# Hybrid decoder layer: hi and lo of the sample tokens in one stationary operand, first two FFN products between the transposes, value products after the gate piece

## The chip, the cores and the metric

The kernel runs on one core of one Trainium2 chip. The metric is device time in microseconds of one launch. TensorE (PE) multiplies matrices into the 8 banks of PSUM; VectorE (DVE), ScalarE (ACT) and GpSimd (POOL) do elementwise work; SyncE's queue (SP) issues most transfers.

## The reference, cut to what matters

One layer over 1024 prompt tokens and 64 sample tokens, D = 1024, all in float32:

```python
x = layer_norm(ALPHA * x + 0.5 * swiglu(x, ffn_wi[0], ffn_wo[0]), ln_g[0], ln_b[0])
q_a, k_a, v_a, q_r, k_r, v_r, g_r, gate_a, gate_b = split(x @ w_in)
o_a = sliding_window_attention(rope(q_a), rope(k_a), v_a, sinks)        # 8 query heads, window 128
o_r = group_norm(retention(rope(q_r), rope(k_r), v_r)) * silu(g_r)      # 4 heads, chunks of 128
merged = sigmoid(gate_a) * (o_a @ w_br_attn) + sigmoid(gate_b) * (o_r @ w_br_ret)
x = layer_norm(ALPHA * x + merged @ w_o, ln_g[1], ln_b[1])
x = layer_norm(ALPHA * x + 0.5 * swiglu(x, ffn_wi[1], ffn_wo[1]), ln_g[2], ln_b[2])
```

`swiglu(x, wi, wo)` is `(silu(x @ wi[:, :F]) * (x @ wi[:, F:])) @ wo` with F = 2816. The sample tokens have a cache and a state of their own and share all weights.

## The kernel before, in words

Matrix products in float32 accuracy are made of three reduced-precision matmuls: both operands are split into a high part (a rounding copy, on ScalarE) and a low part (the difference, on VectorE), and `three` (L1790) issues hi by hi, hi by lo and lo by hi into one bank. So each operand costs ScalarE and VectorE a step, and each product TensorE three passes.

The order of work is written out by hand on every engine, and engines meet by semaphores. Three parts follow each other.

FFN 0 (`ffn(0)` on each engine). The tokens are two halves of 512 (tile p and tile p+4), D is two halves too, and each up projection is seven products of half-size blocks instead of eight (a Strassen-like scheme). Seven blocks of x are needed, numbers 0 to 6: 0, 2 and 6 are parts of x, and 4, 3, 1, 5 are sums that GpSimd makes in `tm` (`combos`, L705). In the head TensorE transposes them p by p (`combos`, L1809, 28 groups of four 128x128 transposes), ScalarE copies the high part, VectorE makes the low part, all through rotating banks. `sample_combos` does the 64 sample tokens. Then come 11 units g of seven products (`up_product`, L1861; two banks of 12 matmuls of 512 columns each), whose results VectorE and ScalarE combine to the two halves of the hidden layer (`up_step`), while `w_hi`, `w_lo` and `w_sum` split and add the weights for the product three ahead in three slots. In unit 0 product 0 uses wa11, product 1 the sum ws2 and product 2 wa12. The sample tokens of products 0, 2, 4 and 5 already use a stationary operand of hi and lo side by side (`sample_product`), added afterwards by a product with `fold`. The hidden layer is spilled, and 77 down steps follow.

The mixer goes over three groups G of tokens: tiles 0 to 2, 3 to 5, and 6, 7 and the 64 sample rows. `build_timeline` lists its stages: P (q, k, v of one retention head, 4 weight pieces), G and G2 (its gate), TR (transposes of q and k), SKV, PVQ, SU (states), T, B (branch product), GB and GA (gates, a piece each, transposed), KVA and QA (attention's projections), AS (scores), EX, FIN (softmax), AP (transposes of the probabilities), AV (value products), A (branch), WO (output product, 2 pieces, added into y by VectorE), LNS and LNH (LayerNorm's statistics; the scaled rows). Weight pieces pass through three raw slots and four split slots (`Pace`). P, G, KVA and QA are `token_major` (L1986): the tokens are the stationary operand, and the third tile of group 2 has only 64 columns.

FFN 1 repeats FFN 0. All engines wait for the last WO piece before it; TensorE waits also for all its additions (`wacc_done`). Its x comes from LayerNorm 1, whose affines of tiles 6, 7 and 8 are VectorE's (`affine`, L1164) and stand between its low parts; those of tiles 0 to 5 are GpSimd's and are done within groups 1 and 2.

## Time and profile before

| | us |
|---|---|
| median of 3 runs (2507.74 to 2508.51) | 2508.28 |
| the profiled execution | 2506.91 |
| its span | 2505.1 |
| TensorE busy | 2434.7 (97%) |
| VectorE busy | 1652.3 (66%) |
| ScalarE busy | 902.5 (36%) |
| GpSimd busy | 232.5 (9%) |

FFN 0 takes the span to about 742 us, the mixer to 1740.6, FFN 1 the rest. A row of a timeline gives start, time, engine, line, operation, out<-in, shapes and, in brackets, how long the engine was idle before it and what released it. A shape `128*64 128x512` is a stationary operand of 128 rows and 64 columns, and 512 moving columns. A matmul's time is a modelled end, the distance of two starts is the pace. Starts are in us from the span's begin.

### The profile page before, as it was taken

To read this page: it belongs to the slowest core of one execution; us is meant where nothing else is said; L and a number is where in the kernel's file an instruction comes from. 1 tells how busy PE (TensorE), PEld (TensorE's weight loads), DVE (VectorE), ACT (ScalarE), POOL (GpSimd) and SP (SyncE) were. 2 spreads that over 40 slices of the span, in tenths; PEclk is the share of its full clock that TensorE was granted. 3 is DMA by queue.
4 is the path that set the end of the run, shared out by engine and by line. 5 is a ranking of instruction groups with operands and counts; after the bars stand their busy time and mean duration, and the time that the engine had idled before them with its cause. 6 is when DMAs were issued, how large, how long until landed. Compare 5 with 4: busy or idle time off the path is not lost.

```text
span 2505.1 us, 31982 instructions
## 1 busy us (share of the span) xinstructions
PE 2434.7 (97%) x12781; PEld 2078.1 (83%) x12781; DVE 1652.3 (66%) x2249; ACT 902.5 (36%) x1280; POOL 232.5 (9%) x306
## 2 busy tenths in 40 slices
PE   7999999999999999999999999998799999999997
PEld 6888888888888898988989778887688888888886
DVE  5666565657886657675666766566765666555788
ACT  4222222243353337442355322373322222224344
POOL 3000000000021000030000221201300000000011
PEclk9999999999999999999999999999899999999999
DMA  4232222266444333333333445424123222227643
GB/s 140 85 120 81 94 80 96 94 225 208 147 138 126 93 101 115 105 114 118 93 115 102 127 128 173 148 85 143 55 84 106 84 105 81 93 85 232 200 147 126
DMA packets 225571, 300.09 MB, mean 120 GB/s; under 512 B 13392, under 2 KB 166272, under 8 KB 222592
## 3 DMA queue, kind: packets, MB, share of 16 engines
q1 hardware_dynamic: 211792, 240.43, 30.4%
q0 software_dynamic: 13056, 56.48, 6.1%
q8 instruction: 101, 1.65, 0.3%
q10 hardware_dynamic: 576, 1.15, 0.1%
q14 instruction: 46, 0.38, 0.0%
HBM read 243.81 MB, written 55.18 MB: 119 GB/s over the span
## 4 chain that ended last, share of the span: by engine, by line
PE 85%; DVE 6%; ACT 3%; issue 2%; POOL 2%; DMA 1%; SPq 0%; DVEq 0%; ACTq 0%; POOLq 0%
PE ps L1794 25%; PE ps L1795 25%; PE ps L1796 25%; PE ps L1849 2%; PE ps L1850 2%; DMA b_raw<-in_ffn_wo 1%; PE ps L1930 1%; PE ps L1931 1%; ACT prob L1075 1%; DVE w_lo L445 1%; ACT w_hi L439 1%; PE ps L1858 1%; DVE b_lo L1253 1%; PE ps L2224 1%; PE ps L2089 0%
## 5 line engine op out<-in xcount | busy, mean ns | idle before, releaser
L1794 PE MATMUL ps<-xc_hi,u_hi 128*128 128x512 f32 x1232 | 483.4, 392 | 0.0
L1795 PE MATMUL ps<-xc_lo,u_hi 128*128 128x512 f32 x1232 | 480.6, 390 | 0.0
L1796 PE MATMUL ps<-xc_hi,u_lo 128*128 128x512 f32 x1232 | 480.1, 390 | 0.0
L445 DVE TENSOR_TENSOR w_lo<-raw,w_hi 128x1024 fp32r<-128x1024 f32 x198 | 253.7, 1295 | 139.8 <-ACT w_hi L439 139.6
L1796 PEld LDWEIGHTS ps<-xc_hi,u_lo 128*128 128x128 f32 x1232 | 231.6, 188 | 49.3
L1794 PEld LDWEIGHTS ps<-xc_hi,u_hi 128*128 128x128 f32 x1232 | 232.0, 188 | 46.1 <-issue 0.2
L1795 PEld LDWEIGHTS ps<-xc_lo,u_hi 128*128 128x128 f32 x1232 | 232.0, 188 | 45.2
L439 ACT ACTIVATE w_hi<-raw 128x1024 fp32r<-128x1024 f32 x198 | 205.7, 1055 | 170.0 <-PE ps L1796 144.8
L1794 PE MATMUL ps<-w_hi,xg_hi 128*128 128x512 f32 (+1 forms) x720 | 246.4, 342 | 1.7 <-issue 1.7
L1794 PE MATMUL ps<-b_hi,h_hi 128*128 128x512 f32 x616 | 241.4, 392 | 2.6 <-DVE b_lo L1253 2.6
L1795 PE MATMUL ps<-w_lo,xg_hi 128*128 128x512 f32 (+1 forms) x720 | 242.0, 336 | 0.0
L1796 PE MATMUL ps<-w_hi,xg_lo 128*128 128x512 f32 (+1 forms) x720 | 241.5, 335 | 0.0
L1796 PE MATMUL ps<-b_hi,h_lo 128*128 128x512 f32 x616 | 239.8, 389 | 0.0
L1795 PE MATMUL ps<-b_lo,h_hi 128*128 128x512 f32 x616 | 239.7, 389 | 0.0
L835 ACT ACTIVATE u_hi<-wa 128x1024 fp32r<-128x1024 f32 x88 | 93.1, 1058 | 303.5 <-PE ps L1850 224.0
L881 ACT ACTIVATE h_hi<-h_raw 128x512 fp32r<-128x512 f32 x154 | 97.3, 632 | 269.6 <-PE ps L1796 185.7
L1213 DVE TENSOR_TENSOR u_lo<-wa,u_hi 128x1024 fp32r<-128x1024 f32 x88 | 109.6, 1246 | 96.8 <-ACT u_hi L835 96.7
L1252 DVE TENSOR_TENSOR h_lo<-h_raw,h_hi 128x512 fp32r<-128x512 f32 x154 | 105.7, 686 | 70.4 <-ACT b_hi L835 70.1
L1794 PEld LDWEIGHTS ps<-w_hi,xg_hi 128*128 128x128 f32 x720 | 131.8, 183 | 20.5 <-issue 3.7
L1796 PEld LDWEIGHTS ps<-w_hi,xg_lo 128*128 128x128 f32 x720 | 131.8, 183 | 17.0
L1795 PEld LDWEIGHTS ps<-w_lo,xg_hi 128*128 128x128 f32 x720 | 131.9, 183 | 16.2
L1794 PEld LDWEIGHTS ps<-b_hi,h_hi 128*128 128x128 f32 x616 | 115.6, 188 | 31.9 <-DVE b_lo L1253 6.6
(289 smaller groups left out, 4451.9 us busy)
## 6 DMA issues: line engine op xcount, KB each, us to landing
raw<-in_w_in SPq DMA_DIRECT2D x90, 512.0 KB, 3.8
wa<-in_ffn_wi SPq DMA_DIRECT2D x88, 512.0 KB, 3.6
h_raw<-h_spill SPq DMA_DIRECT2D x154, 256.0 KB, 2.8
h_spill<-tm POOLq DMA_DIRECT2D x22, 1024.0 KB, 4.1
b_raw<-in_ffn_wo SPq DMA_DIRECT2D x66, 256.0 KB, 3.8
raw<-in_w_in SPq DMA_DIRECT2D x96, 128.0 KB, 2.3
raw<-in_w_in SPq DMA_DIRECT2D x48, 256.0 KB, 3.0
raw<-in_w_br_ret SPq DMA_DIRECT2D x24, 512.0 KB, 3.7
```

The costliest lines, as they stand in the source:

```text
L439: nc.scalar.activation(wslot(n, False), raw[:, s * D:(s + 1) * D], ACT.Copy).then_inc(hi_ready, 1)
L445: nc.vector.tensor_tensor(wslot(n, True), raw[:, s * D:(s + 1) * D], fr(wslot(n, False)), ALU.subtract).then_inc(lo_ready, 1)
L835: nc.scalar.activation(dst, src, ACT.Copy).then_inc(sem_, 1)
L881: nc.scalar.activation(h_hi[s][:], h_raw[s][:], ACT.Copy)
L1075: ins = nc.scalar.activation(pb[:, q * wd:(q + 1) * wd], pb[:, q * wd:(q + 1) * wd], ACT.Exp, bias=nmx[:, s0 + q:s0 + q + 1], accum_out=rs ...
L1213: tt(u_lo[s][:], w_src[i][:], fr(u_hi[s][:]), ALU.subtract).then_inc(u_dve, 1)
L1252: tt(h_lo[s][:], h_raw[s][:], fr(h_hi[s][:]), ALU.subtract)
L1794: mm(out, a_hi, b_hi, start=first, stop=False)
L1795: mm(out, a_hi, b_lo, start=False, stop=False)
L1796: return mm(out, a_lo, b_hi, start=False, stop=last)
L1849: mm(out, lhs, u_hi[s][:, k * 2 * P:(k + 1) * 2 * P], start=first and k == 0, stop=False)
L1850: ins = mm(out, lhs, u_lo[s][:, k * 2 * P:(k + 1) * 2 * P], start=False, stop=last and k == 3)
```

## The change

1. Sample pairs in the mixer. The split x of the sample tile gets its low part also beside the high part (columns 64 to 127 of `xg_hi`, likewise `mT_hi`). `token_major` and WO then issue two matmuls with these 128 columns (by the high and by the low weights), and rows 64 to 127 of the bank are added to rows 0 to 63 by VectorE: `fold_halves`, a copy and an addition, ahead of each use of the sample rows in P, G2, KVA, QA; in WO a second addition. The copy of v in P is made tile by tile behind `rope_src`, and for the sample rows by VectorE.
2. FFN heads. The blocks are now 0, 1 and 6 as parts of x (p, second half is block 1) and 4, 3, 2, 5 as sums; product 1 uses wa12 and product 2 the sum ws2. Blocks 0 and 1 are "early", the others "late", each kind with banks of its own. In FFN 0 the head is the order `HEADS[0]`: E early, L late blocks of p, U one half (12 matmuls) of product 0 or 1. GpSimd's sums have two sets of buffers and wait only for those of p-2. The sample products of 0 and 1 come in the middle of product 2. Loads come in a new order.
3. FFN 1. The early blocks are stages EB of the timeline between the WO stages of group 2, with the first weight split as UW; GpSimd's sums for p of 0 and 1 are made there. LayerNorm's statistics follow each addition of the last WO. The head is `HEADS[1]`, with `affine(1, 6)`, `(1, 7)` and `(1, 8)` behind low parts.
4. AV stands behind the gate piece and EX; in group 0 the four affine steps of P stand ahead of the weight splits.
5. Buffers lie elsewhere in SBUF, with the waits that this needs; one is in the load of down step 2.

```diff
-BLOCKS = (0, 2, 6, 4, 3, 1, 5)
+EARLY = (0, 1)
+LATE = (6, 4, 3, 2, 5)
+HEADS = ((("E", 0), ("E", 1), ("L", 0), ("E", 2), ("E", 3), ("L", 1), ("U", 0), ("U", 1), ("L", 2), ("U", 2), ("U", 3), ("L", 3)),
+         (("E", 0), ("E", 1), ("E", 2), ("E", 3), ("U", 0), ("L", 0), ("U", 1), ("L", 1), ("U", 2), ("U", 3), ("L", 2), ("L", 3)))
+E_BANKS, L_BANKS = (0, 1, 3, 4), (4, 5, 6, 7)
...
-            s += [("AS", u + 2), ("AV", u)] + gate() + [("EX", u + 2)]
+            s += [("AS", u + 2)] + gate() + [("EX", u + 2), ("AV", u)]
...
-        s += [("WO", 1), ("WO", 2), ("WO", 3)] + [("LNS", t) for t in range(3)] + [("LNH", t) for t in range(3)]
+        s += [("WO", 1), ("EB", 0), ("EB", 1), ("WO", 2), ("EB", 2), ("EB", 3), ("UW", 0), ("WO", 3)]
...
+                if t == 2:
+                    sp.wait_ge(prod_done, product(f, UNITS - 1, 6))
...
-                if p:
-                    pool.wait_ge(xb_done, 28 * f + 7 * p)
+                if p >= 2:
+                    pool.wait_ge(xb_done, blocks_made(f, LATE[-1], p - 2))
...
-                if k and kind != "WO" and (kind, x) not in (("A", 0), ("A", 1), ("A", 2)):
-                    pace.stage(n, k)
                 if G == 0 and (kind, x) in (("P", 1), ("P", 2), ("P", 3)):
                     for t in ((NT - 1, 4), (5, 6), (7,))[x - 1]:
                         affine_scale(0, t)
                         affine_shift(0, t)
+                if k and kind != "WO" and (kind, x) not in (("A", 0), ("A", 1), ("A", 2)):
+                    pace.stage(n, k)
...
+            def fold_halves(dst, b, off, n):
+                lo, hi = halves(b, off, n)
+                link(nc.vector.tensor_copy(dst, lo))
+                return tt(dst, dst, hi, ALU.add)
...
+                    for t in range(3 if G < NG - 1 else 2):
+                        R = rows_of(3 * G + t)
+                        act.wait_ge(rope_src, 3 * g + t + 1)
+                        dst = v_r[0:R, (3 * (g % 2) + t) * DV:(3 * (g % 2) + t + 1) * DV]
+                        ins = nc.scalar.activation(dst, bank(t, R, 2 * DK, DV), ACT.Copy)
...
+                        if R == SR:
+                            fold_halves(v_r[0:SR, (3 * (g % 2) + 2) * DV:(3 * (g % 2) + 3) * DV], t, 2 * DK, DV)
+                            src = tA[0:SR, 2 * DK:4 * DK]
+                            link(fold_halves(src, t, 0, 2 * DK))
...
+                            if R == SR:
+                                out, pair = bank(b0 + t, P, 0, width), xg_hi[:, a:a + 2 * SR]
+                                mm(out, pair, wh[:, kk * width:(kk + 1) * width], start=k == 0, stop=False)
+                                ins = mm(out, pair, wl[:, kk * width:(kk + 1) * width], start=False, stop=k == KT - 1)
+                                continue
...
+                        ins = stt(ysl, ysl, ALPHA if x == 0 else 1.0, bank(b, R), ALU.mult, ALU.add)
+                        if R == SR:
+                            link(ins)
+                            ins = tt(ysl, ysl, halves(b, 0, BANK)[1], ALU.add)
+                        ins.then_inc(wacc_done, 1)
+                        if last_group and x == 3:
+                            dve.wait_ge(wacc_done, 24 * G + 18 + q + 1)
+                            ins = nc.vector.bn_stats(st6[0:R, 12 * t + 6 * (q % 2):12 * t + 6 * (q % 2) + 6], ysl)
...
+                else:
+                    late(f, 0)
+                    w_lo(f, 0, 1)
                     affine(1, 6)
+                    late(f, 1)
                     affine(1, 7)
...
+                w_sum(f, 0, 0)
+                late(f, 2)
+                late(f, 3)
+                w_lo(f, 0, 2)
+                first_gate(f)
                 if f:
                     affine(1, 8)
...
+            def head(f):
+                for kind, x in HEADS[f]:
+                    if kind == "E" and f == 0:
+                        early(f, x)
+                    elif kind == "L":
+                        late(f, x)
+                    elif kind == "U":
+                        first_half(f, x // 2, x % 2)
+                sample_combos(f)
+                pe.wait_ge(xb_lo, 28 * (f + 1))
```

## Rows read from the trace of the kernel before

**Rows 1.** The page: busy time of TensorE, share of the span, instructions.

```profile
PE 2434.7 (97%) x12781; PEld 2078.1 (83%) x12781; DVE 1652.3 (66%) x2249; ACT 902.5 (36%) x1280; POOL 232.5 (9%) x306
```

**Rows 2.** Busy times by stretch: us, then PE, PEld, DVE, ACT, POOL, granted clock, DMA.

```profile
6.30:31.90 25.60, 19.62 (x121) 17.03 (x121) 19.60 (x28) 16.53 (x29) 20.98 (x16) 0.87 0.59 202
1401.00:1740.60 339.60, 332.11 (x2095) 276.70 (x2095) 214.62 (x355) 128.84 (x201) 56.76 (x67) 0.98 0.45 140
1740.60:1795.50 54.90, 35.11 (x176) 29.09 (x177) 44.58 (x55) 25.11 (x40) 27.99 (x25) 0.81 0.14 44
```

**Rows 3.** Waits of TensorE, whole span: us in total, times, longest.

```profile
PE ps L2224 <- ACT probT L1086: 6.3, 7, 2.5
...
PE ps L2053 <- ACT v_r L993: 4.4, 3, 1.5
```

**Rows 4.** TensorE by form in 1401 to 1741, the hi-by-hi third: busy us, mean ns.

```profile
L1794 PE MATMUL ps<-w_hi,xg_hi 128*64 128x512 f32 x40 | 15.9, 397 | 0.0
...
L1794 PE MATMUL ps<-w_hi,xg_hi 128*64 128x256 f32 x40 | 11.1, 277 | 0.0
...
L1794 PE MATMUL ps<-w_hi,mT_hi 128*64 128x512 f32 x16 | 6.3, 393 | 0.0
```

**Rows 5.** Timeline of TensorE, group 2, end of P(0) and begin of its transposes.

```profile
1416.76 0.39 PE L1796 MATMUL ps<-w_hi,xg_lo 128*128 128x512 f32 x1
1416.98 0.40 PE L1794 MATMUL ps<-w_hi,xg_hi 128*64 128x512 f32 x1
1417.22 0.39 PE L1795 MATMUL ps<-w_lo,xg_hi 128*64 128x512 f32 x1
...
1421.80 0.28 PE L1796 MATMUL ps<-w_hi,xg_lo 128*64 128x256 f32 x1
1421.92 0.84 PE L2053 MATMUL ps<-ident,qk 128*128 128x128 f32 x4
```

**Rows 6.** Timeline of VectorE in group 2: sample rows of P(0), a state update, WO.

```profile
1419.23 0.41 DVE L1501 TENSOR_TENSOR tA<-ps,cs_ret 64x256 f32<-64x256 f32 x1
1419.57 0.41 DVE L1502 TENSOR_TENSOR tB<-ps,cs_ret 64x256 f32<-64x256 f32 x1
...
1501.18 1.22 DVE L1619 SCALAR_TENSOR_TENSOR st<-st,ps 128x1024 f32<-128x1024 f32 x1 [1.45 <-PE ps L2115]
...
1739.24 0.68 DVE L1163 SCALAR_TENSOR_TENSOR y<-y,ps 64x512 f32<-64x512 f32 x1 [0.69 <-PE ps L1796]
```

**Rows 7.** Timeline of ScalarE in the attention of group 2.

```profile
1648.92 1.00 ACT L1086 ACTIVATE probT<-ps 128x1024 f32<-128x1024 f32 x1
1649.94 1.28 ACT L1032 ACT_TABLE_LOAD   x1
...
1656.02 1.00 ACT L1086 ACTIVATE probT<-ps 128x1024 f32<-128x1024 f32 x1
```

**Rows 8.** Waits of TensorE in 760 to 900.

```profile
PE ps L1794 <- DVE racc L1637: 1.6, 1, 1.6
```

**Rows 9.** Timeline of VectorE in P(1) of group 0.

```profile
784.99 1.23 DVE L445 TENSOR_TENSOR w_lo<-raw,w_hi 128x1024 fp32r<-128x1024 f32 x1 [2.85 <-ACT w_hi L439]
786.13 1.21 DVE L1184 TENSOR_TENSOR y<-y,ln_g_down 64x1024 f32<-64x1024 f32 x1
```

**Rows 10.** Timeline of TensorE: product 2 of FFN 0, WO(2), product 2 of FFN 1.

```profile
45.29 0.39 PE L1794 MATMUL ps<-xc_hi,u_hi 128*128 128x512 f32 x1
...
1724.02 0.39 PE L1794 MATMUL ps<-w_hi,mT_hi 128*128 128x512 f32 x1
...
1795.55 0.39 PE L1794 MATMUL ps<-xc_hi,u_hi 128*128 128x512 f32 x1
```

**Rows 11.** Timeline of GpSimd: a sum in each FFN head.

```profile
7.46 1.28 POOL L722 TENSOR_TENSOR tm<-y 128x512 f32<-128x512 f32 x1
...
1754.46 2.29 POOL L722 TENSOR_TENSOR tm<-y 128x512 f32<-128x512 f32 x1
```

**Rows 12.** Timeline of VectorE: affine of tiles 6 and 7 in the second head.

```profile
1754.41 1.22 DVE L1174 TENSOR_TENSOR y<-y,ln_g_mix 128x1024 f32<-128x1024 f32 x1
...
1757.76 2.28 DVE L1174 TENSOR_TENSOR y<-y,ln_g_mix 128x1024 f32<-128x1024 f32 x1
```

More of the change, by code:

```diff
@@ L184, in slot_of, with block_order, block_place, blocks_made @@
     return n % MSLOTS
+def block_order(f):
+    return [(ci, p) for kind, p in HEADS[f] for ci in {"E": EARLY, "L": LATE, "U": ()}[kind]]
+def block_place(f, ci, p):
+    return block_order(f).index((ci, p))
+def blocks_made(f, ci, p=None):
+    return 28 * f + 1 + max(block_place(f, ci, u) for u in (range(4) if p is None else (p,)))
+def block_bank(ci, p):
+    return E_BANKS[(2 * p + ci) % 4] if ci in EARLY else L_BANKS[(5 * p + LATE.index(ci)) % 4]
+def bank_freed(f, ci, p):
+    n = block_place(f, ci, p)
+    same = [m for m, (c2, p2) in enumerate(block_order(f)[:n]) if block_bank(c2, p2) == block_bank(ci, p)]
+    return 28 * f + same[-1] + 1 if same else 0
 def product(f, g, i):
@@ L501, in down_bank, with halves @@
             return (4 * q + i) % 7
+        def halves(b, off, n):
+            return bank(b, SR, off, n), ps[SR:2 * SR, b * BANK + off:b * BANK + off + n]
         def sample_heads(dst):
@@ L1151, in xT_evac @@
                 lo = dst_lo[:].rearrange("p (k c) -> p k c", c=width)[:, :, col:col + R]
-                tt(lo, pair, hi, ALU.subtract).then_inc(xT_lo_ready, 1)
+                ins = tt(lo, pair, hi, ALU.subtract)
+                if R == SR:
+                    beside = dst_hi[:].rearrange("p (k c) -> p k c", c=width)[:, :, col + SR:col + 2 * SR]
+                    ins = tt(beside, pair, hi, ALU.subtract)
+                ins.then_inc(xT_lo_ready, 1)
             def ln_stats(t):
@@ L1491, in _, with rope @@
             nc.vector.memset(va_prev[:], 0.0).then_inc(prev_zeroed, 1)
-            def rope(G, R, src, t, cs, half, heads, dst1, dst2):
+            def fold_halves(dst, b, off, n):
+                lo, hi = halves(b, off, n)
+                link(nc.vector.tensor_copy(dst, lo))
+                return tt(dst, dst, hi, ALU.add)
+            def rope(G, R, src, t, cs, half, heads, nth=0):
                 cos = cs[0:R, t * 2 * half:t * 2 * half + half]
@@ new lines, in early, with late, first_half @@
+            def early(f, p):
+                if f and p == 0:
+                    pe.wait_ge(m_ready, KT * NG)
+                for ci in EARLY:
+                    block(f, ci, p)
+            def late(f, p):
+                if f and p == 0:
+                    pe.wait_ge(wacc_done, 24 * NG)
+                for ci in LATE:
+                    block(f, ci, p)
+            def first_half(f, i, half):
+                if half == 0:
+                    pe.wait_ge(u_dve, weight_op(f, 0, LO_AT[i]))
+                    pe.wait_ge(xb_lo, blocks_made(f, i))
+                    if f and i == 0:
+                        pe.wait_ge(wacc_done, 24 * (NG - 1) + 21)
+                b = (2, 0)[i] + half
+                for k in range(4):
+                    c0 = k * 2 * P + half * P
+                    xs = slice(k * HALF, (k + 1) * HALF)
+                    ins = three(bank(b), u_hi[i][:, c0:c0 + P], u_lo[i][:, c0:c0 + P],
+                                xc_hi[i][:, xs], xc_lo[i][:, xs], k == 0, k == 3)
+                if half:
+                    ins.then_inc(main_done, 1)
@@ L1891, in up_product @@
                                     xc_hi[i][:, xs], xc_lo[i][:, xs], k == 0, k == 3)
[L1892 to L1893 removed]
+                    if g == 0 and i == 2 and j == 0:
+                        pe.wait_ge(xs_dve, 4 * f + 4)
+                        for first in range(2):
+                            sample_product(f, 0, first).then_inc(prod_done, 1)
+                if i in (0, 1, 4, 5):
+                    if i == 0:
                         pe.wait_ge(fs_ready, u)
[L1895 to L1897 removed]
                     ins = sample_product(f, g, i)
@@ L2301, in _ @@
                             a = mb + f2 * TG + t * P
+                            if R == SR:
+                                out, pair = bank([2, 5, 6, 7][(6 * x + q) % 4]), mT_hi[:, a:a + 2 * SR]
+                                mm(out, pair, wslot(n + f2, False)[:, half * 512:(half + 1) * 512], start=f2 == 0, stop=False)
+                                ins = mm(out, pair, wslot(n + f2, True)[:, half * 512:(half + 1) * 512], start=False, stop=f2 == 1)
+                                continue
                             ins = three(bank([2, 5, 6, 7][(6 * x + q) % 4], R), mT_hi[:, a:a + R], mT_lo[:, a:a + R],
@@ L2307, in _ @@
                     ins.then_inc(piece_used, 2)
-            pe.wait_ge(wacc_done, 24 * NG)
+                elif kind == "EB":
+                    early(1, x)
             ffn(1)
```

370 lines of the change are left out of this document (224 added, 146 removed).

## Prediction, made before the result was known

> **What bounds the kernel now.** I read the page's busy shares first, then busy times by stretch, then TensorE's waits, then the engines' own timelines inside the stretches with gaps. TensorE is busy 97% of the span [rows 1], so time can be saved in two ways: fewer TensorE instructions, or its gaps. The gaps are few. The waits name them [rows 3]: the value products of the attention wait for the copy of the transposed probabilities (6.3 us), the retention transposes for the value copy (4.4 us), and the rest lies mostly in the two FFN heads. By stretch [rows 2], the first head (6.3 to 31.9) has TensorE busy 19.6 of 25.6 us; the second with its first two products (1740.6 to 1795.5) 35.1 of 54.9 us at a granted clock of 0.81 (a mean of stretches at 1.2 and at 2.4 GHz). Group 2 of the mixer (1401 to 1740.6) is the opposite: 332 of 339.6 us busy, VectorE 215 of them. There a removed TensorE instruction counts in full, and what is added to VectorE has room.
>
> **A. Sample pairs (group 2).** Each k of the 64 sample columns now takes three matmuls (hi by hi, lo by hi, hi by lo). The change puts hi and lo side by side as 128 stationary columns and does it in two. By form there are 40 triples 512 wide (four P stages and QA), 40 of 256 (G, G2, KVA) and 16 in WO [rows 4]. The width of the stationary operand doesn't show in the pace: with 128 columns the next matmul starts after 0.22 us, with 64 after 0.24, and at 256 wide after 0.12 [rows 5]; I take 0.23 and 0.12. Saved: 40 x 0.23 + 40 x 0.12 + 16 x 0.23 = 17.7 us.
> The price is on VectorE: the two halves of PSUM are added, a copy and an addition for each tile, of 64 rows. The nearest rows are 0.41 us for 64x256, starting 0.34 apart, and 0.68 for 64x512 [rows 6]. P gets four such steps with four linked waits, about 1.9 us ahead of the third rope. At head 0 only the G piece stands between P and the transposes: P ends near 1417.6, the transposes begin at 1421.9 [rows 5], and the third rope, of 1.3 us, began at 1419.23 [rows 6], with TensorE's stretch between them shorter by 4 x 0.12 us afterwards. I put 1.2 us of stall there. In the other heads the row product and its sample half also lie between (6 us of room). The fold behind G2 (0.8 us) falls into the 1.45 us in which VectorE waits for the state product [rows 6]. KVA, QA and the transposes of x have a stage between them and their readers. Bounds of the stall: nothing, and 3 us if every sample evacuation leaked a little. A = 17.7 - 1.2 = 16.5 (14.5 to 17.7).
>
> **B. Value products behind the gate.** AP, AS, AV, gate, becomes AP, AS, gate, AV. The gate (3.5 us in group 2) covers ScalarE's copy. But ScalarE is the limit there in group 2: between its copies at 1648.92 and 1656.02, 7.1 us, its rows name no idle time, and two table loads of 1.28 us lie there [rows 7]; TensorE's work in such a round is some 6.3 us, worked out from its starts. What the gate hides at the first units comes back in part at AV of the last, when the copy is behind the sample's exponentials (about 1.2 us). Of 3.8 us of gaps in group 2 I keep 2.6, in groups 0 and 1, with longer gates, 1.5 each. B = 5.6; bounds 0 (all given back to ScalarE's chain) and 7.2 (all gaps).
>
> **C. Group 0: affines ahead of the splits, value copies tile by tile.** In P(1) VectorE does four affine steps of 1.21 us from 786.13 on, after the last weight split and before the first rope [rows 9], so the transposes wait. Ahead of the splits they have P's 16 us to hide in; the split they delay (772.4 to 778.4) is used at 783.4. That ends two of the three 1.5 us waits, and the third (head 0) gets 0.8 from the earlier copy. With VectorE 4.9 us earlier some of the branch products' wait for racc (1.6, [rows 8]) goes, I take 0.8. C = 1.6 + 1.6 + 0.8 + 0.8 = 4.8; bounds 1.5 and 6.5.
>
> **D. First FFN head.** Now: 112 transposes in 13.7 us of TensorE time and 6 us of gaps, product 0, a wait for the sample's low parts, its sample product, product 1; product 2 starts at 45.3 [rows 10]. Then: the four halves of products 0 and 1 (12 x 0.23 = 2.7 us each) lie between the blocks. GpSimd's 16 sums (1.28 each, starting 1.25 apart from 6.2, [rows 11]) end near 28 to 30, since they no longer wait for buffers. TensorE: E0 to L1 until about 18.7, U0 and U1 to 24.2, L2 26.6, U2 and U3 32.0, L3 34.4; low parts and the split of ws2 behind it until 36.9. Product 2 starts at 37, one more sample product (1.1 us) comes after it, and the wait for the sample's low parts (until about 40.7, half a product in at 39.7) costs 1.0. Saved 45.3 - 39.1 = 6.2 at most. If the low clock falls into products and not, as now, on transposes (before: a mean of 0.87 in the head [rows 2]), up to 3.4 us of work at half pace go off. D = 5; bounds 1 and 8.
>
> **E. Second FFN head.** The eight early blocks move into WO (32 transposes, 3.7 us of TensorE), LayerNorm's statistics into the last WO, and four halves of products fill the wait for LayerNorm. From the end of WO(1) (1724.0) to product 2 (1795.55) are 71.5 us now [rows 10]. The new limit is VectorE. Behind WO(1) I count on it: 12 additions of 0.62, 4 second halves, 4 splits, 8 early low parts, one u_lo, six statistics; it ends 26.5 us after WO(1), some 7 us after TensorE, which waits 2.9 us before L0. Then five low parts 3.3, u_lo 1.2, affine of 6 2.4, five 3.2, affine of 7 2.4, two weight sums 2.5, ten low parts 6.5, u_lo 1.2, first gate 1.2, affine of 8 2.4: 26.3. GpSimd's sums for p of 2 and 3 cannot start before those affines. Where both engines ran from SBUF in the trace, VectorE's affine took 2.28 us where it is 1.22 alone and GpSimd's sum 2.29 where it is 1.28 [rows 11, 12]; low parts, which read PSUM, kept their 0.6 in the same stretch. That adds 1.6 + 2 us, and the first blocks of L0 and of the last L some 1. Product 2 starts 57.8 us after WO(1); with one more sample product and 0.7 of stall 59.5, so 12.0 us less, of which 1.8 are A's. TensorE idles about 8 us just before product 2; before, its clock was at 1.2 GHz after gaps of 5.3, 4.9 and 2.35 us, and product 1 began at half pace. I take off 2.2. E = 12.0 - 1.8 - 2.2 = 8; bounds 2 and 14.
> The Trainium skill's page "SBUF — State Buffer", section "SBUF: two separate sides", has a rule against this part: a VectorE instruction with two SBUF inputs and a GpSimd one exclude each other for the whole instruction. The rows agree with about one instruction's wait for each meeting. If every one of the five VectorE instructions beside the sums waited once more, E would be 6 and not 8.
>
> **What costs nothing.** In the units g of 1 and above products 1 and 2 swap roles; banks, sums and splits are as many, and TensorE is full there now. The wait put before the load of down step 2 holds SyncE's queue until product 5 of the last unit is through; the step is used 5 us after product 6, and the load takes 3; if that cover went, each such wait is below 3 us. The spills and weight loads of FFN 1 have the WO stretch.
>
> **Sum.** 16.5 + 5.6 + 4.8 + 5 + 8 = 39.9 us off a span of 2505.1; the profiled execution took 2506.91, the runs' median is 2508.28, 1.4 above it, so 2508.3 - 39.9 = 2468.4.
>
> **Rivals.** (1) VectorE and GpSimd hold the heads: D and E give 1 and 2 and not 13. For it: VectorE is busy 44.6 of the 54.9 us of the second head [rows 2], and the slowed pairs. Against: half of its list overlaps products. 2508.3 - 29.9 = 2478.4 and, with a B of nothing, 2484. Chance 0.15. (2) The pair doesn't save: a full stationary operand costs 3/2 of a half one. Then A is -1 and the time 2486. Against it are the equal spacings of rows 5. 0.03. (3) The heads close wholly (D 8, E 14, C 6.5): 2456. 0.12. (4) Slower: the sample evacuations on VectorE put TensorE on hold. The place is group 2: 4 P, 4 G2, 8 WO, KVA and QA, 18 places. From 39.9/18 = 2.2 us of stall at each on the kernel is slower; at 3 us it takes 2522. Against: each is 0.8 to 1.9 us long and 17 of the 18 have a stage behind them. 0.03. The forecast has 0.67.
> The likeliest case with its neighbours spans 2458 to 2480; to hold 8 in 10 I give 2456 to 2484. 0.2% (5 us) is about what a measurement of this kernel tells from no change: faster 0.96, same 0.01, slower 0.03.
>
> **What would show it.** In group 2 no third matmul and some 17 us less; one wait of about 1 us before the transposes of head 0, none at the others. No wait of AV for probT in groups 0 and 1. Waits on v_r gone at heads 1 and 2. Product 2 at 35 to 40 us; from the end of WO(1) to product 2 55 to 61 us, with VectorE unbroken and TensorE idle before it. Wrong if waits for VectorE's folds appear in group 2, if WO grows, or if TensorE's granted clock is low over more than 20 us of the second head.

## The result, and the profile after

The changed kernel takes 2484.8 us (2482.3 to 2490.2, four runs), the kernel before 2508.0 on the same chip: a ratio of 0.991 (95% interval 0.9894 to 0.9926, as for all ratios below), 23 us less where 39.9 were forecast, and 0.8 us beyond the upper end of the range. The profiled execution of after is its slowest, 2490.2 us with a span of 2487.9; its place in the spread comes up below.

The page's first row, beside [rows 1]: TensorE has 96 fewer instructions on record and 12 us less busy time, but it is busy for the same 97%.

```profile
PE 2422.7 (97%) x12685; PEld 2074.8 (83%) x12685; DVE 1672.0 (67%) x2292; ACT 901.3 (36%) x1295; POOL 234.2 (9%) x306
```

Busy times by stretch, columns as in [rows 2]: first head, group 2 up to WO, WO of group 2, second head up to product 2.

```profile
6.30:31.90 25.60, 20.78 (x120) 18.11 (x121) 20.89 (x26) 15.15 (x27) 23.80 (x16) 0.93 0.59 202
1391.10:1695.05 303.95, 290.52 (x1848) 250.41 (x1849) 199.66 (x352) 121.02 (x192) 56.82 (x67) 0.95 0.43 132
1695.05:1737.38 42.33, 38.02 (x186) 30.41 (x185) 40.75 (x56) 12.72 (x18) 11.55 (x10) 1.00 0.50 174
1737.38:1775.05 37.67, 25.27 (x136) 21.53 (x136) 35.63 (x43) 17.49 (x26) 15.36 (x16) 0.86 0.12 42
```

TensorE's waits of the whole span, to be read beside [rows 3]: the v_r wait is gone. In its place stand waits for VectorE that the kernel before does not have: for qk ahead of head 0's transposes (L2267), for the decayed sample keys (L2329), for the additions in WO (L2518), for the sample tile's affine in the second head (L2050). (`qk` are the rotated queries and keys, `kdec_m` the decayed sample keys, `st` the retention state, `probT` the transposed probabilities.)

```profile
PE ps L1998 <- DVE xc_lo L1289: 8.2, 6, 2.7
...
PE ps L2050 <- DVE y L1270: 6.0, 1, 6.0
PE ps L2267 <- DVE qk L1678: 4.6, 2, 4.3
PE ps L2518 <- DVE y L1258: 2.8, 4, 1.1
...
PE ps L2329 <- DVE kdec_m L1735: 2.5, 1, 2.5
```

In the stretches of [rows 2] VectorE had 215 of 340 us to do in group 2; in WO alone it now works 40.75 of 42.33 us. The wait at L2267 is longer than in any of the repeats below. The chain behind it, rows of ScalarE, VectorE (two) and TensorE: the split of a weight piece waits for its load, rope waits behind the split, the transposes for rope.

```profile
1406.36 1.06 ACT L475 ACTIVATE w_hi<-raw 128x1024 fp32r<-128x1024 f32 x1 [4.59 <-DMA raw<-in_w_in]
...
1407.45 1.23 DVE L481 TENSOR_TENSOR w_lo<-raw,w_hi 128x1024 fp32r<-128x1024 f32 x1 [4.42 <-ACT w_hi L475]
1408.59 0.42 DVE L1631 TENSOR_TENSOR tA<-ps,cs_ret 128x256 f32<-128x256 f32 x1
...
1414.35 0.47 PE L2267 MATMUL ps<-ident,qk 128*128 128x128 f32 x1 [4.33 <-DVE qk L1678]
```

Rope (the rotation of queries and keys) of the first tile starts at 1408.59, though TensorE's P ended at 1406.03, where the G piece's first matmul starts: it lies behind the split. From there to the transposes VectorE works without a gap, 5.8 us with four fold instructions of 0.45.

Where the time went, from the starts of TensorE's stages, in us. "Group 2" runs from the first WO matmul of group 1 to the first of group 2, "low" is the part of it in which the granted clock was 1.2 and not 2.4 GHz, "WO to product 3" ends where product 3 of the second FFN starts; e0 to e11 are the experiments.

| | group 2 | low | less low/2 | wait for kdec_m | WO | WO to product 3 |
|---|---|---|---|---|---|---|
| before | 343.6 | 10.2 | 338.5 | none | 36.1 | 97.9 |
| after, first profile | 344.2 | 30.7 | 328.8 | 2.5 | 41.5 | 88.9 |
| e0 after again | 335.9 | 17.1 | 327.4 | 2.5 | 41.5 | 88.8 |
| e1 state load later | 336.2 | 17.1 | 327.6 | 2.5 | 41.6 | 89.1 |
| e2 also all affines later | 345.1 | 30.7 | 329.7 | none | 41.6 | 89.3 |
| e3 no pairs | 339.8 | 6.8 | 336.3 | none | 39.7 | 84.9 |
| e4 WO unpaired | 339.7 | 23.9 | 327.7 | 2.5 | 39.7 | 85.0 |
| e5 same, group 2's affines late | 333.9 | 17.1 | 325.4 | none | 39.7 | 84.7 |
| e6 no folds in P | 333.1 | 13.7 | 326.3 | 1.0 | 41.5 | 89.2 |
| e7 tiny sums | 337.6 | 20.5 | 327.4 | 2.5 | 39.4 | 85.1 |
| e8 L3 before U3 | 336.2 | 17.1 | 327.7 | 2.5 | 41.5 | 88.9 |
| e9 best | 330.3 | 10.2 | 325.1 | none | 39.7 | 82.0 |
| e10 no pairs, affines late | 341.3 | 10.2 | 336.2 | none | 39.7 | 84.9 |
| e11 best again | 333.5 | 17.1 | 325.0 | none | 39.7 | 82.0 |

(WO of before has none of the early blocks in it, so its 36.1 is not to be set beside the others.) The fourth column takes off half of the low time, what a stretch at half pace costs a TensorE that never pauses. It turns scattered numbers into levels: 338.5 before, 336.2 and 336.3 without pairs, 327.4 to 328.8 with them, 325.0 to 325.4 with pairs and late affines (e2 and e6, which change waits in between, stand apart). Most of the scatter is the clock.

### The profile page after: what moved, and what is told of

The parts are those of the page before. It is cut to its first block, busy times and chain, and to the rows that moved or that the text cites. A ratio compares the mean times of both kernels' runs of the same rounds, so it can differ in the third digit from the quotient of the medians.

```text
span 2487.9 us, 31860 instructions
## 1 busy us (share of the span) xinstructions
PE 2422.7 (97%) x12685; PEld 2074.8 (83%) x12685; DVE 1672.0 (67%) x2292; ACT 901.3 (36%) x1295; POOL 234.2 (9%) x306
## 4 chain that ended last, share of the span: by engine, by line
PE 83%; DVE 10%; ACT 3%; issue 2%; DMA 1%; POOL 0%; SPq 0%; DVEq 0%; ACTq 0%
PE ps L1968 24%; PE ps L1969 23%; PE ps L1970 23%; DVE w_lo L481 2%; PE ps L2063 2%; PE ps L2062 2%; DVE y L1258 1%; PE ps L2140 1%; ACT w_hi L475 1%; PE ps L2141 1%; DVE xc_lo L1289 1%; PE ps L2071 1%; PE ps L1998 1%; DMA raw<-in_w_in 1%; PE ps L2303 1%
## 5 line engine op out<-in xcount | busy, mean ns | idle before, releaser
L1968 PE MATMUL ps<-w_hi,xg_hi 128*128 128x256 f32 (+1 forms) x640 | 221.3, 346 | 1.7 <-issue 1.7
L1969 PE MATMUL ps<-w_lo,xg_hi 128*128 128x256 f32 (+1 forms) x640 | 216.9, 339 | 0.0
L1970 PE MATMUL ps<-w_hi,xg_lo 128*128 128x256 f32 (+1 forms) x640 | 216.7, 339 | 0.0
L894 ACT ACTIVATE u_hi<-ws 128x1024 fp32r<-128x1024 f32 x66 | 70.0, 1060 | 257.4 <-PE ps L1970 152.2
L1968 PEld LDWEIGHTS ps<-w_hi,xg_hi 128*128 128x128 f32 x640 | 122.8, 192 | 17.1 <-issue 3.7
L1970 PEld LDWEIGHTS ps<-b_hi,h_lo 128*128 128x128 f32 x616 | 115.6, 188 | 24.3
```

Source lines behind the costliest of these rows:

```text
L894: nc.scalar.activation(dst, src, ACT.Copy).then_inc(sem_, 1)
L1968: mm(out, a_hi, b_hi, start=first, stop=False)
L1969: mm(out, a_hi, b_lo, start=False, stop=False)
L1970: return mm(out, a_lo, b_hi, start=False, stop=last)
```

## The experiments

**First: which of the waits, and what are the pairs worth?** e0 is the changed kernel itself.

> The changed kernel as it is, on the same chip as the three that follow, for their comparison. Theory (waits, then clock): group 2 of the mixer gained nothing because TensorE waits 4.4 us ahead of head 0's transposes and 2.5 us ahead of head 0's state product, and the granted clock stands at 1.2 GHz right behind each wait; so the 1.2 GHz stretches lie at the same places again (1413 to 1420 and 1450 to 1454 us of the profile). Rival (the clock falls by chance): the stretches lie elsewhere and their sum differs by several us from the 30.7 us of the first profile, with the waits unchanged. Median 2485 for both.

Measured: 2483.3 us (2482.8 to 2483.8), ratio 0.9894 (0.9879 to 0.9909). The wait ahead of head 0's transposes is 0.9 us here, not 4.3; the one for kdec_m is 2.5 again; the low stretch at 1413 is missing, the one behind the kdec_m wait is there (1447.4 to 1450.8). So neither theory had it whole: a low stretch goes with a wait, and the long wait at head 0 was this one execution's. The last weight piece of P(0) and G came late there: ScalarE waited 4.59 us for its load, in e0 1.18, and the split starts at 1405.54 in e0 although that group begins 1.7 us later. Rows of ScalarE and VectorE in e0:

```profile
1404.45 1.06 ACT L475 ACTIVATE w_hi<-raw 128x1024 fp32r<-128x1024 f32 x1 [1.18 <-DMA raw<-in_w_in]
1405.54 1.23 DVE L481 TENSOR_TENSOR w_lo<-raw,w_hi 128x1024 fp32r<-128x1024 f32 x1 [1.01 <-ACT w_hi L475]
```

Group 2 takes 335.9 us and not 344.2, which is why the first profile is the slowest run.

e1, against the load collision:

```diff
-                elif kind == "P" and G == NG - 1 and x == 0:
+                elif kind == "TR" and G == NG - 1 and x == 0:
                     pool.wait_ge(piece_used, n)
                     pool.dma_start(st[:].rearrange("p (b e) -> p b e", b=DB),
```

> One change: head 0's state load (1 MB, from GpSimd's queue) is issued when the P and G pieces of head 0 in group 2 are used, at about 1414 us, and not at 1399.1 beside a load of the weights. Theory (waits, then clock): the weights land some 4 us earlier, the split is out of VectorE's way, the wait ahead of head 0's transposes falls from 4.4 to 1 to 1.5 us, and the 6.8 us at 1.2 GHz behind it go: 3 us of the wait and 3.4 us of clock, 2478 to 2480. Rival (the wait only moves to the next reader, or the load isn't its cause): within 1 us of the kernel of the first run.

Measured: 2484.0 us (2482.6 to 2491.3), ratio 0.9903 (0.9886 to 0.992); the wait is 1.3 us. The theory falls: the load of the state isn't what held the split in the general run, since e0 with the old place waits 0.9.

e2, e1 with all of GpSimd's LayerNorm affines moved:

```diff
-    if G:
-        s += [("LNH-", t) for t in range(3)]
...
     s += [("MB", f) for _, f in first]
+    if G:
+        s += [("LNH-", t) for t in range(3)]
```

> The state load as in the run before, and the LayerNorm affines of a group's previous tiles (GpSimd, six of 2.2 us) moved from head 0 of groups 1 and 2 to behind the GB pieces' merge. Theory (waits, then clock): VectorE's rope of head 1 starts at the end of its P stage and not 2.6 us later, so the 2.5 us wait for the decayed keys and the 3.4 us at 1.2 GHz behind it go too: another 4 us, 2474 to 2476. Rival (the folds on VectorE make the waits, whatever GpSimd does): the 2.5 us stay, within 1 us of the run before.

Measured: 2502.6 us (2499.1 to 2508.5), ratio 0.9974 (0.9964 to 0.9983), 19 us slower than e0. The part it was made for came true. In e0 VectorE's splits lie beside the affines; the first two rows below are VectorE's, the next two GpSimd's, the last TensorE's:

```profile
1423.62 12.88 DVE L481 TENSOR_TENSOR w_lo<-raw,w_hi 128x1024 fp32r<-128x1024 f32 x4 [3.06 <-ACT w_hi L475]
...
1437.19 1.67 DVE L1677 TENSOR_TENSOR qk<-tA,tB 128x128 f32<-128x128 f32 x1
...
1428.83 3.26 POOL L731 TENSOR_TENSOR y<-y,ln_b_mix 128x1024 f32<-128x1024 f32 x1
1432.05 3.36 POOL L730 TENSOR_TENSOR y<-y,ln_g_mix 128x1024 f32<-128x1024 f32 x1
...
1444.81 0.48 PE L2329 MATMUL ps<-v_r,kdec_m 32*128 32x256 f32 x2 [2.46 <-DVE kdec_m L1735]
```

Four splits take 12.88 us, 3.2 each, and a qk step of 0.29 takes 1.67. In e2, with no affine there, a split takes 1.23 and rope starts at the end of its P stage:

```profile
1442.39 1.23 DVE L481 TENSOR_TENSOR w_lo<-raw,w_hi 128x1024 fp32r<-128x1024 f32 x1 [2.40 <-ACT w_hi L475]
1443.81 0.42 DVE L1631 TENSOR_TENSOR tA<-ps,cs_ret 128x256 f32<-128x256 f32 x1 [0.19 <-PE ps L1970]
```

The wait for kdec_m and the low stretch behind it are gone. But the affines now lie where VectorE makes the rotated queries, and TensorE waits there instead, once in group 1 (e2, TensorE's waits between 1068 and 1363, below) and twice in group 2 (3.6 and 5.2 us), with stretches of 6.8 us at 1.2 GHz beside all three. Groups 1 and 2 are longer than in e0 by 9.9 and 9.1 us, which is the loss:

```profile
PE ps L2395 <- DVE qa L1828: 8.2, 1, 8.2
```

The place decides, not the amount. The Trainium skill's page "SBUF — State Buffer", section "SBUF: two separate sides", says that a VectorE instruction with two SBUF inputs and a GpSimd one that reads SBUF exclude each other at the ports that they share: whichever starts first holds them for its whole length. The splits here agree with that (1.23 alone, 3.2 beside affines, whose steps take 2.4 alone): each lost about what one affine step takes.

e3, the pairs undone in P, G, KVA, QA and WO, everything else kept:

```diff
-                            if R == SR:
-                                out, pair = bank(b0 + t, P, 0, width), xg_hi[:, a:a + 2 * SR]
-                                mm(out, pair, wh[:, kk * width:(kk + 1) * width], start=k == 0, stop=False)
-                                ins = mm(out, pair, wl[:, kk * width:(kk + 1) * width], start=False, stop=k == KT - 1)
-                                continue
...
-                            link(ins)
-                            ins = tt(ysl, ysl, halves(b, 0, BANK)[1], ALU.add)
```

> The changed kernel without the sample tokens' pairs: three products of 64 columns' rows each time, no fold and no second half, all else kept. The prediction's price for the pairs was 16.5 us, so 2501. Theory (waits, then clock): group 2 lost as much to waits and to the clock as the pairs saved there (about 14 us), and only WO's 3.6 us are left: 2486 to 2490. Rival (pairs save nothing on TensorE by themselves): 2485, with P stages of group 2 as short as with pairs.

Measured: 2483.7 us (2481.9 to 2486.6), ratio 0.99 (0.9883 to 0.9916). **The pairs, 16.5 us of the forecast, are worth 0.4 us by the medians, nothing that these runs tell from zero.** (The intervals of the two ratios, 4 us to each side, leave no room for 16.5.) That is even less than the waits theory allowed. But its rival (they save nothing by themselves) is wrong too: from its first matmul's start to its last one's, P takes 14.5 us with them and 16.5 without. e0 above, e3 below, columns as in [rows 2]: group 2 up to WO, WO, and 4 us behind the kdec_m wait of e0.

```profile
1393.00:1688.48 295.48, 285.40 (x1848) 246.96 (x1848) 199.58 (x351) 120.86 (x192) 56.81 (x67) 0.97 0.44 135
1688.48:1730.80 42.32, 38.04 (x186) 30.38 (x184) 40.74 (x56) 12.71 (x18) 11.53 (x10) 1.00 0.51 174
...
1447.00:1451.00 4.00, 4.00 (x21) 3.99 (x21) 3.17 (x7) 1.71 (x3) 2.18 (x5) 0.57 0.46 131
```

```profile
1391.80:1691.07 299.27, 294.35 (x1927) 247.71 (x1928) 186.64 (x319) 122.27 (x197) 56.84 (x67) 0.99 0.44 133
1691.07:1730.98 39.91, 39.91 (x202) 31.39 (x201) 36.08 (x49) 12.97 (x19) 13.57 (x11) 1.00 0.53 185
...
1447.00:1451.00 4.00, 4.00 (x33) 3.77 (x34) 3.57 (x8) 1.72 (x3) 0.56 (x1) 1.00 0.35 118
```

Up to WO the pairs save 8.9 us after the clock is taken off (336.3 against 327.4), the clock takes 5.1 back (17.1 against 6.8 us low in these two profiles; e10, without pairs too, has 10.2), and from WO to product 3 they cost 3.9. The 8.9 can be counted: outside WO the instructions save 14.0 (17.7 less WO's 3.7), and up to WO TensorE idles 10.8 us in e0 and 5.7 in e3, 5.1 more. In WO TensorE without pairs works all of its 39.91 us, with them 38.04 of 42.32, while VectorE is at 40.74: the work went to the engine that had none to spare.

**Second: each loss by itself.** e4 takes the pairs from WO alone (the last two lines of the diff of e3, and WO's matmuls).

> The changed kernel with WO of group 2 alone back at three products for the sample tile, P, G, KVA and QA still in pairs. Theory (the accumulations hold TensorE): in WO a bank comes free only when VectorE has added it to y, the pair needs two 512-column adds there instead of one, and TensorE waits 4 to 5 us at WO's sample tiles; so without the pair WO takes 39.7 us as in the kernel without any pairs, and not 41.5, product 0 to product 1 of the second FFN takes 13 us and not 15.4 since VectorE is less behind, and the kernel takes 2479. Rival (the prediction's 3.6 us saved in WO, hidden by something else): 2487.

Measured: 2483.4 us (2481.9 to 2484.2), ratio 0.9898 (0.9883 to 0.9913). The stages did what was expected, WO 39.7, product 0 to product 1 12.9, and WO to product 3 85.0 instead of 88.8. The time did not move, since group 2 ahead of WO had 23.9 us of low clock and not 17.1 in this profile (3.4 us), though the edit lies behind it. So a gain of 3.8 us is seen in the stages and is not shown in the time. What held WO in e0 is seen in VectorE's groups by form between 1688 and 1731, and in TensorE's row of the first wait:

```profile
L1258 DVE SCALAR_TENSOR_TENSOR y<-y,ps 128x512 f32<-128x512 f32 x15 | 9.7, 674 | 0.0
...
L1924 DVE TENSOR_TENSOR y<-y,ps 64x512 f32<-64x512 f32 x6 | 4.1, 690 | 0.2
...
1707.27 0.50 PE L2518 MATMUL ps<-w_hi,mT_hi 128*128 128x512 f32 x1 [1.12 <-DVE y L1258]
```

A second addition costs as much as the first one, 0.69 us, and a bank comes free only behind it. Eight of them (six in this window) are 5.5 us of VectorE against 3.7 of TensorE. Four low parts beside the high ones (L1905, 0.43 us each) come on top.

e5 adds to e4 the late place for group 2's three affines, beside the sample tokens' value products:

```diff
-    if G:
+    if G and not last:
         s += [("LNH-", t) for t in range(3)]
...
-        s += [("SP", 0), sigmoid()] + gate() + [("SV", 0)]
+        s += [("SP", 0), sigmoid()] + gate() + [("LNH-", t) for t in range(3)] + [("SV", 0)]
```

> As the run before, and group 2's three LayerNorm affines on GpSimd moved from head 0's G2 and head 1's P stage to the sample tokens' value products, where VectorE is busy 2.2 to 2.6 us in 10. Theory (waits, then clock): the 2.5 us wait for the decayed keys at 1442 us goes, as in the run with all affines moved, and the 3.4 us at 1.2 GHz behind it; nothing waits elsewhere, 4.2 us less than the run before, 2475. Rival (a wait of like size comes elsewhere, at the sample attention or at the tail): within 1 us of the run before.

Measured: 2475.6 us (2473.8 to 2476.9), ratio 0.9867 (0.9853 to 0.9882): 7.8 less than e4, where 4.2 were expected. The kdec_m wait and the low stretch behind it are gone, nothing new waits, and group 2 is 5.7 us shorter: 2.3 of it waits, 3.4 the clock. So about half of the gain is the clock's. This is the first kernel clearly better than the changed one.

e6 leaves out the second halves in P (three of the four fold instructions, and with them the low parts of the sample tokens' queries, keys and values), and e7 cuts GpSimd's sums to 8 columns (the sum blocks are then transposed from x itself, so the sums are missing from both FFNs):

```diff
-                            fold_halves(v_r[0:SR, (3 * (g % 2) + 2) * DV:(3 * (g % 2) + 3) * DV], t, 2 * DK, DV)
-                            src = tA[0:SR, 2 * DK:4 * DK]
-                            link(fold_halves(src, t, 0, 2 * DK))
+                            nc.vector.tensor_copy(v_r[0:SR, (3 * (g % 2) + 2) * DV:(3 * (g % 2) + 3) * DV], bank(t, SR, 2 * DK, DV))
```

> The changed kernel with the second halves of the P pieces' pairs left out: rope reads the first half from its bank, and one copy instead of copy and add goes to the values, so three of four fold instructions of each P stage (1.35 us) are gone and the sample tokens' low parts are missing from queries, keys and values. Theory (folds and GpSimd's affine together): VectorE is 1.35 us and more earlier at head 1's decayed keys, the 2.5 us wait shrinks to 1 us or less, the wait ahead of head 0's transposes to 0, 2480. Rival (GpSimd's affine alone makes the wait): it keeps 2 us or more, 2483.

Measured: 2483.9 us (2483.5 to 2484.9), ratio 0.9902 (0.9887 to 0.9917). The waits go as the theory said, for kdec_m from 2.5 to 1.0, ahead of head 0's transposes to none; a wait for the state at the next product is 2.6 where e0 has 1.4, so part is only handed on. The time is that of e0: group 2 gained 1.1 us after the clock, and this profile lost 3 us in the first FFN (mixer start at 745.5, e0 742.7), where it has 6.8 us at 1.2 GHz about product 2's begin. Folds and affines make the kdec_m wait together: with the affines and no fold at all it is gone (e3), with the folds and no affine it is gone (e2, e5), and with the affines and one of four folds 1.0 us is left.

```diff
-                nc.gpsimd.tensor_tensor(s[0], b12, b11, sub).then_inc(xb_sum, 1)
+                nc.gpsimd.tensor_tensor(s[0][:, 0:8], b12[:, 0:8], b11[:, 0:8], sub).then_inc(xb_sum, 1)
```

> The changed kernel with GpSimd's 32 sums of x blocks in the two FFN heads cut from 512 to 8 columns, and the sum blocks transposed from x itself: the FFNs' combination inputs are wrong, TensorE's, ScalarE's and VectorE's instructions are all there. Theory (GpSimd and VectorE slow each other in the heads): VectorE's weight splits and low parts take 1.1 to 1.3 us and not 1.85 to 2.3, product 2 of the first FFN starts at 37 to 38 us and not 42.3, and the second head, product 0 to product 2, shrinks from 37.3 to 33 us: 2475. Rival (banks and VectorE's own work hold the heads): product 2 at 41 or later, the second head within 1 us, 2482.

Measured: 2478.0 us (2476.3 to 2481.4), ratio 0.9879 (0.9863 to 0.9896). Product 2 of the first FFN starts at 40.3, 2.0 us earlier, not the 5 that the theory claimed, and 1.2 of the 2.0 lie between the starts of products 0 and 1, where e0 has its low stretch of 3.4 us (20.6 to 24.1); e7 has its one behind product 2's begin (40.9), and its last up product starts only 1.2 us earlier. The second head, product 0 to product 2, takes 34.9 and not 37.3, WO 39.4 and not 41.5. So GpSimd's sums cost 3.7 us from WO to product 3 (85.1 for 88.8), and some 1 us in the first head, where 5.3 are missing (37 forecast, 42.3 measured).

**Third: the heads, and the pairs once more.** e8 swaps two entries:

```diff
-HEADS = ((("E", 0), ("E", 1), ("L", 0), ("E", 2), ("E", 3), ("L", 1), ("U", 0), ("U", 1), ("L", 2), ("U", 2), ("U", 3), ("L", 3)),
+HEADS = ((("E", 0), ("E", 1), ("L", 0), ("E", 2), ("E", 3), ("L", 1), ("U", 0), ("U", 1), ("L", 2), ("U", 2), ("L", 3), ("U", 3)),
```

> The changed kernel with one swap in the first FFN's head: the last late blocks (L3) are transposed ahead of product 1's second half (U3), not behind it. In the profile VectorE is idle from 34 to 38 us (busy 0.04 of 4 us) and then works 4 us while TensorE stands until product 2 at 42.3. Theory (the order leaves VectorE's low parts behind the last plain product): product 2 starts at 39.5 to 40, the last up product ends 2.5 us earlier, 2481. Rival (banks: L3's four banks aren't free until L2's low parts are made, so TensorE waits as long before U3): product 2 at 42, 2483.5.

Measured: 2480.0 us (2478.0 to 2481.9), ratio 0.9892 (0.9876 to 0.9909). Product 2 starts at 39.6, the last up product at 500.3 instead of 503.2. In e0 VectorE idles while TensorE runs U2 and U3, and works while TensorE stands; in e8 it works beside TensorE. Columns as in [rows 2], e0 first:

```profile
34.00:38.00 4.00, 4.00 (x25) 3.48 (x24) 0.04 (x1) 0.67 (x2) 0.00 (x0) 1.00 0.00 0
38.00:42.30 4.30, 1.94 (x18) 1.37 (x17) 4.30 (x7) 2.93 (x7) 0.00 (x0) 1.00 0.00 0
```

```profile
36.60:39.60 3.00, 3.00 (x19) 2.26 (x17) 2.97 (x5) 0.36 (x1) 0.00 (x0) 1.00 0.00 0
```

The medians' difference, 3.3 us, fits the 2.9 of the stages; the ratios (0.9892 and 0.9894) do not tell the two apart, so this gain too is seen in the stages alone.

e9 is e5 with that swap, and the sample tokens' transposes in the middle of product 2, their products behind it, in both heads:

```diff
                     if g == 0 and i == 2 and j == 0:
-                        pe.wait_ge(xs_dve, 4 * f + 4)
-                        for first in range(2):
-                            sample_product(f, 0, first).then_inc(prod_done, 1)
+                        sample_combos(f)
+                if g == 0 and i == 2:
+                    pe.wait_ge(xs_dve, 4 * f + 4)
+                    sample_product(f, 0, 0).then_inc(prod_done, 1)
+                    sample_product(f, 0, 1).then_inc(prod_done, 2)
+                    return
```

> WO unpaired and group 2's affines late (the 2475.6 us kernel), with L3 ahead of U3 in the first head and, in both heads, the sample tokens' eight transposes moved from ahead of product 2 into its middle, so that product 2 no longer waits behind the sample tile's affine on VectorE (TensorE stands from 1753.4 to 1760.05 us there). Theory: 2.5 us in the first head and 4 us in the second, 2469. Rival (VectorE, busy without a gap from 1731 to 1762 us, delivers the sample combinations as late as before and TensorE waits for them behind product 2): second head 0 to 1 us, 2473.

It aims at these rows of e5, where product 2 (third row) has its last split at 1756.5, 4.6 us before it starts, and stands behind transposes that wait for an affine:

```profile
1753.01 0.66 PE L1992 MATMUL ps<-ident,tm_odd 128*128 128x128 f32 x4
1760.05 1.11 PE L2044 MATMUL ps<-ident,y 64*128 64x64 f32 x8 [6.37 <-DVE y L1270]
1761.09 0.79 PE L1962 MATMUL ps<-xc_hi,u_hi 128*128 128x512 f32 x1
```

Measured: 2473.1 us (2469.0 to 2478.6), ratio 0.9864 (0.9848 to 0.9881). e11, the same kernel again:

> The kernel of the run e9 once more, in five rounds, to narrow its interval: its four times lay between 2469.0 and 2478.6 us. Theory (waits taken away, 1.2 GHz stretches after them gone): median 2469 to 2473, below the 2475.6 us of the kernel without the two changes of the heads, and in the profile no wait of 2 us or more in group 2. Rival (the gain of the heads is given back to the clock): 2475 to 2476, with as much time at 1.2 GHz as there (46 us).

Measured: 2472.2 us (2469.5 to 2475.0), ratio 0.9853 (0.9834 to 0.9872). Product 2 starts 17.7 us behind product 1 and not 22.2, but product 3 follows 11.5 later and not 9.6, since the sample combinations are late then: 2.7 us remain at product 3 (82.0 against 84.7). The waits of e11 between 1389 and 1770:

```profile
PE ps L1992 <- DVE xc_lo L1289: 4.9, 3, 2.7
PE ps L1962 <- DVE u_lo L1330: 4.5, 2, 2.9
...
PE ps L2263 <- DVE qk L1678: 1.0, 1, 1.0
```

So the truth lies between theory and rival of e9: the wait for the affine (6.4 us in e5) went, and waits for splits (4.5, L1962) came on a VectorE without a gap; those for low parts (4.9, L1992) are as in e5 (5.0). TensorE idles 2.0 us less, and 6.8 us lie at 1.2 GHz instead of 13.7.

In the first head the move takes back what the swap gives. With the swap alone (e8) product 3 starts at 47.7 and the last up product at 500.3. In e9 the sample tokens' steps on VectorE stand ahead of the split that product 3 needs (row of TensorE in e9), and the last up product starts at 502.6 (e11 502.2):

```profile
49.90 0.47 PE L1962 MATMUL ps<-xc_hi,u_hi 128*128 128x512 f32 x1 [1.60 <-DVE u_lo L1330]
```

The swap with the transposes moved in the second head alone was not run. The time of e9 and e11 (ratios 0.9864 and 0.9853) isn't told from e5's 0.9867; the kernel is some 11 us faster than the changed one and 37 faster than the one before.

e10 is e3 with group 2's affines late, so it differs from e5 by the pairs of P, G, KVA and QA alone:

> The kernel without any pairs, with group 2's three affines late as in the 2475.6 us kernel: the two differ by the pairs of P, G, KVA and QA alone. Theory (the pairs save what their instructions say, 13 us in group 2, where the waits they raise are taken away): the kernel without pairs has no wait for the decayed keys to lose, so it stays at 2483, and the pairs are worth 7 to 10 us, waits ahead of head 0's transposes and some clock deducted. Rival (the late affines are what pays, pairs or not): 2476 to 2478.

Measured: 2486.5 us (2481.6 to 2487.5), ratio 0.9913 (0.9898 to 0.9927). Its waits for VectorE in group 2 are the old ones; the longest (TensorE's waits from 1393 to 1736):

```profile
PE ps L2295 <- DVE st L1749: 1.5, 1, 1.5
PE ps L2246 <- DVE st L1749: 1.4, 1, 1.4
```

The late affines bring nothing without the pairs (336.2 against 336.3 in the fourth column), and the pairs bring 10.8 us with them in the medians (ratios 0.9913 and 0.9867, intervals apart), 7.4 in group 2's length and 10.8 there after the clock is taken off. That two of these agree is chance: the profile of e10 has 6.8 us at 1.2 GHz in the first head that e5 has not (mixer start at 744.1 against 742.5). Most of the saving was in the kernel all the time, behind a wait, the clock behind it and a WO that couldn't use it.

## Why the prediction was wrong, and where it was right

**C and B: right.** Mixer start to WO of group 0 went from 291.3 to 283.8 us, 7.5 where C and B's first share said 6.3; group 1 from 327.0 to 325.8, 1.2 for 1.5; group 2 by 2.2 after the clock (before against e3), for 2.6 (TensorE's idle time up to WO went from 8.3 to 5.7). No wait of AV is left in groups 0 and 1, the v_r waits of [rows 3] are gone. That the gate covers ScalarE's copy only in part in group 2 was also right: 1.6 us of waits for probT remain.

**A: wrong, 16.5 forecast, 0.4 measured, not told from nothing.** Its instructions are right (0.23 and 0.12 us each: P 14.5 us for 16.5, G 3.8 for 4.2), and rival 2, the dear stationary operand, is out. Three of its steps failed.

- *Who pays in WO.* The price of the sample tile's second addition was counted only as a delay of a reader; WO was in no list of places without a stage between. VectorE had to add 5.5 us to a stage in which e3, without them, already keeps it busy for 36.1 of 39.9 us. WO and the head behind it cost 3.9 us instead of saving 3.7. The E part's own list put additions, splits and low parts of WO on VectorE and found it 7 us late; A took the same time for free. One sum for the engine over both parts would have shown it.
- *The stall.* 1.2 us at head 0 and none elsewhere, with 6 us of room, held at head 0 in the kernels with whole folds (0.9 to 1.6), not in the first profile (4.3), and failed at head 1: 2.5 us for kdec_m. The room there was counted from P's end to its reader. But VectorE reaches P's end late, because GpSimd's affines stretch its splits to 3.2 us, and the folds come on top. The prediction used exactly this collision in E, and not where six affine steps stood in the timeline.
- *The clock.* A was priced at full clock. In the kernels with the 2.5 us wait (after, e0, e1, e4, e7, e8) a stretch at 1.2 GHz begins 1.4 to 2.6 us after that wait's end, six times of six, and in the other profiles none lies there. The next wait, some 10 us on, is for st and in every profile (1.4 us, in e6 2.6): a low stretch begins within 1.6 us of its end in eight (before, after, e2, e4, e6, e7, e10, e11) and in six it does not. So a wait of some us is often paid again, by half of the low stretch (1.7 us for one of 3.4), but which of the short waits are followed by one changes from run to run. Before had 10.2 us low in group 2, after 30.7 in one execution and 17.1 in the next.

**D: wrong, 5 forecast, 1.2 measured** (last up product 504.3, then 503.1 to 503.2; and before had 6.8 us at 1.2 GHz in this head, after 3.4). "Product 2 starts at 37" failed: it starts at 42.2. E0 to L1 end at 21.4 and not 18.7, with u_lo at 1.85 us and waits for banks; most of a low stretch of 3.4 us falls into U0; and L3's low parts, foreseen with the split of ws2 as a tail of 2.5 us, are with it 4.2 us of work that begins only at 37.8, behind U3. The swap of e8 brings 2.9 us at the last up product, taking the sums away 1.2. That more of VectorE's tail lay in the order than in its amount was not seen.

**E: right in its mechanism, its size too small by 5.** WO(1)'s end (1715.8) to product 2 is 59.3 us, forecast 57.8; VectorE is unbroken, and TensorE idles 6 us before product 2, where 8 were forecast. But that is with A's load on VectorE. Without it (e3) WO to product 3 went from 97.9 to 84.9, 13.0 us where E had 8. Of these, 8.2 are idle time; the other 4.8 are the pace, as many matmuls (378 and 379 on record) busy for 73.3 us and not 78.1, with 13.7 us at 1.2 GHz and not 20.5. The prediction took 2.2 us off for a clock that would fall in the longer gap; it was low for less time instead. A's loss and E's surplus hid each other, which kept the milestone in its range of 55 to 61.

**The sum.** By stages, e0 against before: 0.6 us longer to the mixer's start (the last up product is 1.1 earlier, the down steps are 1.7 longer, in a scatter of 237.6 to 239.5 for the changed kernels and 237.8 before), 7.3 shorter to WO of group 0, 1.2 in group 1, 7.7 in group 2 (2.2 of B, 8.9 of A, less 3.4 for the clock), 9.1 from WO to product 3 (13.0 of E, less 3.9 of A), and 0.2 longer behind it: 24.5 us, and the span is 24.4 shorter. So the step that failed is A's: it took a full VectorE and a full clock for free, and of the 14.0 us saved in instructions outside WO the waits left 8.9, the clock 3.8, and WO with the head behind it nothing.

Of the rivals the fourth named the right mechanism, evacuations that hold TensorE, with the wrong price: it takes about 0.2 to 2.5 us at a few of its 18 places, enough to eat A, not the change. The first, VectorE holding the heads, is half true, for D. That its 2484 (with a B of nothing) and the second one's 2486 lie beside the measured 2484.8 is luck: D gave 1, but E 13, B came, and the pairs do save in P. Two slips in the prediction's arithmetic decide nothing: the third rival's terms give 2457.7 and not 2456, and E's list ends at 57.4 and not 57.8. The line "wrong if waits for VectorE's folds appear in group 2, if WO grows" is what came.

**Left open.** What sets the low stretches of the sample attention (6.8 or 10.2 us in each kernel, beginning between 1661 and 1687) was not tried. The 4.3 us at head 0 was seen once, behind a late load of a weight piece; why it was late is open, and e0 and e1 show only that it isn't there with either place of the state's load in a second execution.

## What to carry to other kernels

Halving the small matmuls of a full TensorE is worth its face value only where the engine that must put the halves together has room in that very stage: add up that engine's work by stage, with all parts of the change in one sum. Ask, where VectorE and GpSimd both work from SBUF, which long instructions of the one lie beside the other's chain; with three affines moved to a stretch where VectorE is at 2 in 10, and WO left alone, pairs worth nothing became worth 7 to 11 us. Where edits are judged by 0.2%, read the stages with the clock taken off first; medians alone showed nothing of the 3.8 us that e4's stages gain.

## What the runs showed of the hardware

Where VectorE's steps with two SBUF inputs lay beside GpSimd's affines (e0), a 1.23 us split took 3.2, a 0.29 us qk step 1.67, and an affine step of GpSimd 3.3 instead of 2.4. On a TensorE that is busy 97% of the span the granted clock still fell from 2.4 to 1.2 GHz in or behind single waits of 1.2 us (e9) to 8.2 us (e2), and the same kernel showed 17.1 us of it in one group in one execution and 30.7 in another.
